# Additions of a state-space layer and of an index stage moved from VectorE to GpSimd

## The chip, the cores and the metric

The kernel runs on one core of one Trainium2 chip. The metric is the device time of one execution in microseconds (us). Engines are named as in the profile: PE is TensorE's matmul and PEld its weight load, DVE is VectorE, ACT is ScalarE, POOL is GpSimd, SP is SyncE, which here only issues loads.

## The reference

A decoder trunk of two layers on 256 tokens of width 1024, in float32. Layer 0 mixes with attention and a gating unit, layer 1 with an S5 state-space layer and a GLU; each is followed by a PEER layer of 8 heads with 16 experts a head and token. Cut to what the change touches:

```python
# S5, for every group of 16 channels: 64 complex states, a scan over the tokens
xr = jnp.einsum('bsgc,gpc->bsgp', u, bbr)
xi = jnp.einsum('bsgc,gpc->bsgp', u, bbi)
_, _, sr, si = lax.associative_scan(combine, (a_r, a_i, xr, xi), axis=1)
# PEER: the 16 best pairs of 16 x 16 candidates, as rows of a table of 16384 experts
cand = sv[:, :, 0, :, None] + sv[:, :, 1, None, :]
cidx = si[:, :, 0, :, None] * PEER_NKEYS + si[:, :, 1, None, :]
cs, cpos = lax.top_k(cand.reshape(t, PEER_HEADS, -1), PEER_TOPK)
idx = jnp.take_along_axis(cidx.reshape(t, PEER_HEADS, -1), cpos, axis=-1)
act = gelu(einsum('td,tkd->tk', xbb, u_tab[ib]));  y = einsum('tk,tkd->td', gb * act, v_tab[ib])
```

## The kernel before

Two tiles of 128 tokens, two layers and eight heads give 32 groups of routing and expert work (`GROUPS`), n = 0 to 31, of 16 experts each: 512 steps g. Each engine runs the same list of steps in order. In step g GpSimd gathers one row of 2048 float32 (u and v of one expert) for each of 128 tokens, 1 MB, into one of nine buffers (`RING`, line 463); VectorE multiplies the u half with `h` and sums it (`dot_product`, L1324); ScalarE makes a gate weight and a diagonal of it (L661 to L667); TensorE multiplies the v half with that diagonal (`expert`, L920). The gather of step g waits until the expert of step g - 9 is done (`v_done`).

All other work hangs in a table `WORK`, written out by hand in `between()`: at a step, an engine first runs its part of the stages that stand there and then that step's expert work. Group n's routing begins at step `ROUTE_AT[n]`; `ROUTE` gives the stages' offsets from there (keys 0, pairs 2, best 4, exp 6, index 6, gate 8). S5 works in 8 chunks of 128 channels for each token tile t, nine steps apart, from step 128 (t + 1) + 11: `s5_rot` at slot + 1, `s5_add` at slot + 2, `s5_scan` at slot + 3, `s5_back` at slot + 5, `s5_out` (TensorE) at slot + 6.

- `s5_rot` multiplies the input in PSUM by a table of cosines and one of sines (L1213, L1214), `s5_add` turns them into the real and the imaginary part (L1218, L1219: 128x512 each), `s5_scan` runs two scans (L1231), and `s5_back` turns back (L1240, L1242). All of it is on VectorE, with a drain (VectorE waits until it has finished) between dependent steps.
- `route_index` makes the 16 indices of a group: positions split into row and column (L1298, L1299), a one-hot comparison (L1301), a product with the keys' indices (L1304), a sum over 16 (L1306) and the combination (L1308), which releases `idx_ok`. GpSimd waits for `idx_ok` at the first gather of a group, ScalarE in `q_keep` before it overwrites scores.
- GpSimd has, apart from one mask at the start (L452), only the gathers.

Of the kernel before, what the change touches and what calls it, by code (L numbers as in the profile page):

```python
# [19 lines left out]
ALU = mybir.AluOpType  # L20
# [49 lines left out]

ROUTE = (("route_keys", 0), ("route_pairs", 2), ("route_best", 4), ("route_exp", 6), ("route_index", 6),
         ("route_gate", 8))
ROUTE_AT = {1: 0, 2: 16, 3: 26, 4: 40, 5: 50, 6: 72, 7: 80, 8: 88, 9: 96, 10: 104, 11: 112, 12: 120, 13: 134, 14: 150,
            15: 166, 16: 234, 17: 242, 18: 250, 19: 260, 20: 276, 21: 292, 22: 308, 23: 324, 24: 362, 25: 370, 26: 378,
            27: 400, 28: 416, 29: 432, 30: 448, 31: 464}
ROUTE_ALL = [(name, 0) for name, _ in ROUTE]


PRELUDE = [("norm_T", 0), ("hT_copy", 0), ("norm_sq", 0), ("norm_ms", 0), ("norm_sd", 0), ("norm_r", 0),
# [13 lines left out]
def between():  # L95
# [3 lines left out]
    def at(n, slot, *stages):  # L99
        work[n + slot // TOPK].setdefault(slot % TOPK, []).extend(stages)  # L100
# [57 lines left out]
    for t in range(T):  # L158
        g = PH * (t + 1)
        at(g, 2, ("y_sum", 2 + 2 * t))  # L160
        mix_norm(g, 3, 4 + 2 * t)
        at(g, 3, ("s5_turns", t, 0))
        at(g, 4, ("s5_frac", t, 0))
        at(g, 6, ("s5_tables", t, 0))
        for c in range(KC):
            slot = 11 + 9 * c
            at(g, slot - 1 if c == 0 else slot - 6, ("s5_in", t, c))
            at(g, slot, ("s5_decay", t, c))
            at(g, slot + 1, ("s5_rot", t, c))
            at(g, slot + 2, ("s5_add", t, c))  # L170
            at(g, slot + 3, ("s5_scan", t, c))
            at(g, slot + 4, ("s5_cmat", t, c))
            at(g, slot + 5, ("s5_back", t, c))
            if c + 1 < KC:
                at(g, slot + 3, ("s5_turns", t, c + 1))
                at(g, slot + 4, ("s5_frac", t, c + 1))
                at(g, slot + 6, ("s5_tables", t, c + 1))
            at(g, slot + 6, ("s5_out", t, c))
            if c % 4 == 3:
                at(g, slot + 8, ("s5_gelu", t, c // 4))  # L180
        for b in range(2):
# [24 lines left out]
def trunk(nc, x_in, vecs, cols_in, cst_in, w_in, sgu_g, sgu_wT, sgu_bT, w_out, s5_par, s5_b, s5_c, glu_w, wq, skT, uv_tab,  # L206
          out):
    with ExitStack() as ctx:
# [51 lines left out]
        def part(start, size, pattern="p (a s) -> p a s", **dims):  # L260
# [187 lines left out]
        @block.gpsimd  # L448
        def _(pool):
            pool.wait_ge(ld_sgu, 48)  # L450
            sg3 = sgw[:, :].rearrange("p (h i) -> p h i", h=8)
            nc.gpsimd.affine_select(out=sg3, in_=sg3, pattern=[[0, 8], [1, P]], compare_op=ALU.is_ge, fill=0.0, base=0,  # L452
                                    channel_multiplier=-1).then_inc(sgm_ok, 1)

            for g in range(GROUPS * TOPK):
                n, s = g // TOPK, g % TOPK
                if s == 0:
                    pool.wait_ge(idx_ok, n + 1)
                if g < RING and g % 2 == 0:
                    pool.wait_ge(z_done, 6 + g // 2)  # L460
                if g >= RING:
                    pool.wait_ge(v_done, g - RING + 1)
                nc.gpsimd.indirect_dma_start(  # L463
                    out=ring[g % RING], out_offset=None, in_=uv_tab,
                    in_offset=bass.IndirectOffsetOnAxis(ap=idx[n % AHEAD][:, s:s + 1], axis=0)).then_inc(got[g % RING], 16)

# [478 lines left out]
        def _(dve):  # L945
# [268 lines left out]
                V.tensor_tensor(by_sin, x4, sin, ALU.mult).then_inc(w_ok, 1)  # L1214
                dve.drain()

            def s5_add(t, c):
                V.tensor_tensor(by_cos[:, 0, :, :], by_cos[:, 0, :, :], by_sin[:, 1, :, :], ALU.add)  # L1218
                V.tensor_tensor(by_cos[:, 1, :, :], by_cos[:, 1, :, :], by_sin[:, 0, :, :], ALU.subtract)  # L1219
                dve.drain()  # L1220
                if t == 1:

                    V.tensor_tensor(by_cos[:, :, :, 0], by_cos[:, :, :, 0], z_last[:, :, 4 * c:4 * c + 4], ALU.add)
                    dve.drain()

            def s5_scan(t, c):

                dve.wait_ge(dt5_ok, KC * t + c + 1)
                for r in range(2):
                    w = by_cos[:, r, :, :].rearrange("p j s -> p (j s)")  # L1230
# [19 lines left out]
                xs = x[:, t, cols_]  # L1250
                V.scalar_tensor_tensor(xs, gate[:, cols_], 0.5, xs, ALU.mult, ALU.add).then_inc(x_done, 1)

            hot = cand[:, :].rearrange("p (a k) -> p a k", k=TOPK)
            hot2 = cand[:, :].rearrange("p (i a k) -> p i a k", i=2, k=TOPK)

            def route_keys(n):

# [22 lines left out]
            def route_best(n):  # L1280

                top_cs = cs[n % 2]
                V.max(top_cs[:, 0:8], cand_a)
                V.tensor_scalar(top_f[:, 0, :], top_i[:, 0, :], float(NK * (n // (T * PH))), None, ALU.add)
                V.tensor_copy(top_f[:, 1, :], top_i[:, 1, :])
                dve.drain()
                V.max_index(pos_i[:, 0:8], top_cs[:, 0:8], cand_a)
# [4 lines left out]
                dve.drain()  # L1292
                V.max_index(pos_i[:, 8:16], top_cs[:, 8:16], cand_b).then_inc(cs_ok, 1)
                dve.drain()

            def route_index(n):

                V.tensor_scalar(pos_ab[:, 0, :], pos_i[:, :], 4, None, ALU.logical_shift_right)  # L1298
                V.tensor_scalar(pos_ab[:, 1, :], pos_i[:, :], 15, None, ALU.bitwise_and)  # L1299
                dve.drain()  # L1300
                V.tensor_tensor(hot, bc(pos_ab[:, :, :].rearrange("p i a -> p (i a)"), [None, TOPK]),  # L1301
                                bc(iota16, [2 * TOPK, None]), ALU.is_equal)
                dve.drain()
                V.tensor_tensor(hot2, hot2, top_f[:, :, :].unsqueeze(2).to_broadcast([P, 2, TOPK, TOPK]), ALU.mult)  # L1304
                dve.drain()
                V.tensor_reduce(row[:, :, :].rearrange("p i a -> p (i a)"), hot, AX.X, ALU.add)  # L1306
                dve.drain()
                V.scalar_tensor_tensor(idx[n % AHEAD][:, :], row[:, 0, :], float(NK), row[:, 1, :], ALU.mult,  # L1308
                                       ALU.add).then_inc(idx_ok, 1)

            def route_gate(n):
# [7 lines left out]
            def dot_product(g):  # L1319
# [11 lines left out]
                         s5_frac=s5_frac, s5_add=s5_add, s5_scan=s5_scan, s5_back=s5_back, glu_sum=glu_sum, norm_r=norm_r)  # L1331
            stage |= dict(route_keys=route_keys, route_pairs=route_pairs, route_best=route_best, route_index=route_index,
                          route_gate=route_gate)

            def run(stages):
# [85 lines left out]
```

## Time and profile before

| | |
|---|---|
| median of 3 runs | 1553.74 us (1551.52 to 1554.93) |
| the profiled execution, its own time | 1553.37 us |
| its span, first to last instruction | 1551.6 us |
| busy: PE, DVE, ACT, POOL | 1097.8, 1111.5, 770.2, 589.4 us |
| DMA moved | 603.39 MB, 389 GB/s on average |
| indirect gathers | 512, 536.90 MB, 84.8% of 16 DMA engines' span |

The page gives busy times of the engines, then the span in 40 slices (busy share in tenths, DMA share and GB/s), then the chain that ended last and the costliest groups of instructions. A group's row reads: line, engine, operation, output <- input with shapes, count, busy us in total, mean ns of one, idle time of the engine before them and what ended it.

### The profile page before, as it was taken

How to read it: one execution, taken by the hardware profiler on the slowest of the kernel's cores; microseconds unless marked ns; L12 is line 12 of the kernel's file. 1: busy time of each engine (PE TensorE's matmuls, PEld its weight loads, DVE VectorE, ACT ScalarE, POOL GpSimd, SP SyncE). 2: the span in 40 equal slices, each digit the busy share in tenths (PEclk: the TensorE clock that was granted, in tenths of full speed). 3: DMA queues.
4: the chain of work that ended last, by engine and by line, in shares of the span. 5: the costliest groups of instructions: out<-in, count | busy, mean ns of one | idle time of the engine just before them, and what ended most of it. 6: DMA issues, size and time to landing. Idle time of an engine off the chain costs nothing.

```text
span 1551.6 us, 19133 instructions
## 1 busy us (share of the span) xinstructions
PE 1097.8 (71%) x5920; PEld 348.4 (22%) x5920; DVE 1111.5 (72%) x2533; ACT 770.2 (50%) x2120; POOL 589.4 (38%) x517
## 2 busy tenths in 40 slices
PE   7997678866765666679866575656878666666665
PEld 3542222322211212223221121212323111111110
DVE  2356887479787899985477799999456866666554
ACT  2315554445456667764334666766334644444433
POOL 0024343323443354554334345344432443434430
PEclk9998689878966776879988567686998777676675
DMA  9569999999999998999999999999999999999995
GB/s 358 179 234 413 420 405 418 414 415 408 415 421 421 354 374 358 410 421 415 412 413 414 403 357 369 355 363 406 380 416 415 415 422 421 421 421 421 421 422 234
DMA packets 105418, 603.39 MB, mean 389 GB/s; under 512 B 9314, under 2 KB 9442, under 8 KB 39780
## 3 DMA queue, kind: packets, MB, share of 16 engines
q0 software_dynamic: 73728, 536.90, 84.8%
q1 hardware_dynamic: 31588, 65.26, 11.3%
q8 instruction: 47, 0.77, 0.2%
q14 instruction: 55, 0.45, 0.1%
HBM read 601.08 MB, written 1.05 MB: 388 GB/s over the span
## 4 chain that ended last, share of the span: by engine, by line
DMA 32%; DVE 31%; PE 22%; ACT 7%; issue 3%; DVEq 3%; ACTq 1%; POOL 1%; SPq 0%; POOLq 0%
DMA rings<-in_uv_tab_dram,idx 24%; DVE rings L1324 11%; PE ps L715 9%; PE ps L920 8%; DMA wst<-in_wq_dram 7%; DVE mem L1231 2%; PE ps L908 2%; DVE dgs L1324 2%; ACT dgs L667 1%; DVE mem L1213 1%; ACT wgt L664 1%; DMA rings<-in_w_in_dram 1%; DVE mem L1242 1%; ACT L661 1%; DVE mem L1240 1%
## 5 line engine op out<-in xcount | busy, mean ns | idle before, releaser
L920 PE MATMUL ps<-rings,dgs 64*64 64x512 f32 x3648 | 638.0, 804 | 343.3 <-ACT dgs L667 342.6
L463 POOL DMA_INDIRECT rings<-in_uv_tab_dram,idx x456 | 521.7, 1144 | 804.3 <-PE ps L920 687.8
L1324 DVE CUSTOM_DVE_ANT_0 rings<-rings,h 128x1024 f32<-128x1024 f32 x456 | 550.7, 1224 | 210.8 <-DMA rings<-in_uv_tab_dram,idx 197.7
L661 ACT ACTIVATE gel<-dots 128x1 f32<-128x1 f32 x512 | 102.1, 199 | 522.2 <-DVE dots L1324 518.5
L920 PEld LDWEIGHTS ps<-rings,dgs 64*64 64x64 f32 x3648 | 128.3, 163 | 783.4 <-ACT dgs L667 682.3
L667 ACT ACTIVATE dgs<-cst,wgt 128x128 f32<-128x128 f32 x512 | 205.6, 402 | 36.3 <-issue 1.5
L715 PE MATMUL ps<-wst,hT 128*128 128x512 f32 x320 | 168.0, 666 | 37.1 <-DMA wst<-in_wq_dram 20.5
L664 ACT ACTIVATE wgt<-gel,share 128x1 f32<-128x1 f32 x512 | 150.8, 295 | 35.5 <-issue 0.3
L920 PE MATMUL ps<-dgs 64*64 64x512 f32 x448 | 80.2, 795 | 53.2 <-ACT dgs L667 53.1
L463 POOL DMA_INDIRECT dgs<-in_uv_tab_dram,idx x56 | 65.9, 1176 | 88.3 <-PE ps L920 74.8
L715 PEld LDWEIGHTS ps<-wst,hT 128*128 128x128 f32 x320 | 63.4, 212 | 138.1 <-issue 134.9
L1324 DVE CUSTOM_DVE_ANT_0 dgs<-dgs,h 128x1024 f32<-128x1024 f32 x56 | 68.5, 1223 | 26.5 <-DMA dgs<-in_uv_tab_dram,idx 24.5
L661 ACT ACT_TABLE_LOAD x56 | 71.8, 1283 | 3.8 <-DVE dots L1324 2.2
L715 PE MATMUL ps<-rings,hT 128*128 128x512 f32 x128 | 59.0, 611 | 3.7 <-DMA rings<-in_w_in_dram 2.8
L1324 DVE DVE_READ_ACCUMULATOR2_ANT dots<- 128x1 f32 x512 | 42.6, 83 | 0.0
L648 ACT ACT_TABLE_LOAD x31 | 39.8, 1283 | 0.8
L920 PEld LDWEIGHTS ps<-dgs 64*64 64x64 f32 x448 | 14.2, 156 | 106.9 <-ACT dgs L667 101.2
L1231 DVE TENSOR_TENSOR_SCAN mem<-mem 128x512 f32<-128x512 f32 x32 | 37.4, 1210 | 0.0
L556 ACT ACTIVATE mem<-ps 128x512 f32<-128x512 f32 x16 | 9.5, 594 | 53.6 <-PE ps L715 53.6
L715 PEld LDWEIGHTS ps<-rings,hT 128*128 128x128 f32 x128 | 24.4, 197 | 33.2 <-issue 33.1
L1108 DVE COPY mem<-ps 128x512 f32<-128x512 f32 x16 | 11.0, 689 | 27.4 <-PE ps L707 27.4
L908 PE MATMUL ps<-wst,hT 128*128 128x512 f32 x64 | 29.6, 605 | 0.0
(192 smaller groups left out, 991.2 us busy)
## 6 DMA issues: line engine op xcount, KB each, us to landing
wst<-in_wq_dram SPq DMA_DIRECT2D x15, 2048.0 KB, 28.2
wst<-in_w_out_dram SPq DMA_DIRECT2D x4, 2048.0 KB, 22.8
wst<-in_glu_w_dram SPq DMA_DIRECT2D x4, 2048.0 KB, 31.7
rings<-in_uv_tab_dram,idx POOLq DMA_INDIRECT x456, 15.7
rings<-in_w_in_dram SPq DMA_DIRECT2D x3, 2048.0 KB, 16.7
rings<-in_w_in_dram SPq DMA_DIRECT2D x2, 1024.0 KB, 7.5
dgs<-in_w_in_dram SPq DMA_DIRECT2D x1, 2048.0 KB, 19.4
vec<-in_vecs_dram SPq DMA_DIRECT2D x3, 512.0 KB, 17.2
```

What stands on the lines that cost most here:

```text
L463: nc.gpsimd.indirect_dma_start(out=ring[g % RING], out_offset=None, in_=uv_tab, in_offset=bass.IndirectOffsetOnAxis(ap=idx[n % AHEAD][:, s ...
L648: A.activation(gexp[n % 2][:, :], cs[n % 2][:, :], ACT.Exp, bias=ncs[n % 2], accum_out=gsum[n % 2]).then_inc(exp_ok, 1)
L661: A.activation(gel[i][:, every], dots[i][:, every], ACT.Gelu_apprx_tanh)
L664: A.activation(wgt[i][:, c], gel[i][:, c], ACT.Copy, scale=share[n % AHEAD][:, c])
L667: A.activation(diag[:, (g + k) % DIAGS, :], ident, ACT.Copy, scale=wgt[i][:, c]).then_inc(diag_ok, 1)
L715: ins = PE.matmul(ps[:, bank, :], lhs[:, k, :], rhs[:, k, :], start=(k == 0), stop=(k == KC - 1))
L908: ins = PE.matmul(ps[:, 2 + b, :], hTs[t][:, k, :], wst[:, w % 2, k, :], start=False, stop=(k == KC - 1))
L920: ins = PE.matmul(ps[64 * b:64 * b + 64, 4 + 2 * t + half, :], diag[rows, g % DIAGS, rows], ring[g % RING][rows, D + b * BANK:D + (b + 1) ...
L1213: V.tensor_tensor(by_cos, x4, cos, ALU.mult)
L1231: ins = V.tensor_tensor_scan(w, decay.rearrange("p j s -> p (j s)"), w, 0.0, ALU.mult, ALU.add)
L1240: V.tensor_tensor(by_sin, by_cos, sin, ALU.mult).then_inc(d_ok, 1)
L1324: V.tensor_tensor_reduce(out=u, in0=u, in1=h[:, t, :], scale=1.0, scalar=0.0, op0=ALU.mult, op1=ALU.add, accum_out=dots[n % 2][:, s:s + 1] ...
```

## The change

- `s5_add` moves from VectorE to GpSimd. It waits for `w_ok` (the second product of `s5_rot`), and its second addition increments `add_ok`, for which `s5_scan` now waits. `s5_scan` moves from slot + 3 to slot + 4. The small addition for t = 1 goes into `s5_scan`.
- `route_index` is taken apart. The split of positions and the comparison go to the end of `route_best` on VectorE (two steps earlier). For n > 0 the product is GpSimd's (`index_key`, offset 6), and the sum over 16 becomes four halvings there, of 256, 128, 64 and 32 elements a partition (`index_half`, offset 7; `index_end`, offset 8), then a sum of 16 and a copy to the integer tile. Each of them waits for the semaphore `hop_ok` that the one in front increments. The factor 128 moves to a small operation on VectorE that was there. Group 0 keeps the old form (`route_first`).
- The one-hot tile is a new one, `hot_p`, and `route_best` of group n waits for the indices of group n - 1.
- GpSimd runs the stages of step g - 6 (`POOL_LAG`) in front of the gather of step g.

```diff
+POOL_LAG = 6
-ROUTE = (("route_keys", 0), ("route_pairs", 2), ("route_best", 4), ("route_exp", 6), ("route_index", 6),
-         ("route_gate", 8))
+ROUTE = (("route_keys", 0), ("route_pairs", 2), ("route_best", 4), ("route_exp", 6), ("index_key", 6),
+         ("route_gate", 8), ("index_half", 7), ("index_end", 8))
...
-            at(g, slot + 3, ("s5_scan", t, c))
+            at(g, slot + 4, ("s5_scan", t, c))
...
+            def s5_add(t, c):
+
+                pool.wait_ge(w_ok, KC * t + c + 1)
+                nc.gpsimd.tensor_tensor(by_cos[:, 0, :, :], by_cos[:, 0, :, :], by_sin[:, 1, :, :], ALU.add)
+                nc.gpsimd.tensor_tensor(by_cos[:, 1, :, :], by_cos[:, 1, :, :], by_sin[:, 0, :, :],
+                                        ALU.subtract).then_inc(add_ok, 1)
...
+            def halve(n, step, w):
+
+                pool.wait_ge(hop_ok, 6 * (n - 1) + step)
+                nc.gpsimd.tensor_tensor(hot[:, :, 0:w], hot[:, :, 0:w], hot[:, :, w:2 * w], ALU.add).then_inc(hop_ok, 1)
+
+            def index_key(n):
+
+                pool.wait_ge(pos_ok, n)
+                nc.gpsimd.tensor_tensor(hot2, hot2, top_f[:, :, :].unsqueeze(2).to_broadcast([P, 2, TOPK, TOPK]),
+                                        ALU.mult).then_inc(hop_ok, 1)
+
+            def index_half(n):
+                halve(n, 1, 8)
+                halve(n, 2, 4)
+
+            def index_end(n):
+                halve(n, 3, 2)
+                halve(n, 4, 1)
+                pool.wait_ge(hop_ok, 6 * (n - 1) + 5)
+                nc.gpsimd.tensor_tensor(hot2[:, 0, :, 0], hot2[:, 0, :, 0], hot2[:, 1, :, 0], ALU.add).then_inc(hop_ok, 1)
+                pool.wait_ge(hop_ok, 6 * n)
+                nc.gpsimd.tensor_copy(idx[n % AHEAD][:, :], hot2[:, 0, :, 0]).then_inc(idx_ok, 1)
...
             for g in range(GROUPS * TOPK):
                 n, s = g // TOPK, g % TOPK
+                if g >= POOL_LAG:
+                    run(WORK[(g - POOL_LAG) // TOPK].get((g - POOL_LAG) % TOPK, []))
                 if s == 0:
                     pool.wait_ge(idx_ok, n + 1)
...
-            def s5_add(t, c):
-                V.tensor_tensor(by_cos[:, 0, :, :], by_cos[:, 0, :, :], by_sin[:, 1, :, :], ALU.add)
-                V.tensor_tensor(by_cos[:, 1, :, :], by_cos[:, 1, :, :], by_sin[:, 0, :, :], ALU.subtract)
-                dve.drain()
+            def s5_scan(t, c):
+
+                dve.wait_ge(add_ok, KC * t + c + 1)
                 if t == 1:
...
                 V.max(top_cs[:, 0:8], cand_a)
-                V.tensor_scalar(top_f[:, 0, :], top_i[:, 0, :], float(NK * (n // (T * PH))), None, ALU.add)
+                if n:
+                    dve.wait_ge(idx_ok, n)
+                V.tensor_scalar(top_f[:, 0, :], top_i[:, 0, :], float(NK * (n // (T * PH))), float(NK), ALU.add, ALU.mult)
...
                 V.max_index(pos_i[:, 8:16], top_cs[:, 8:16], cand_b).then_inc(cs_ok, 1)
                 dve.drain()
-
-            def route_index(n):
-
                 V.tensor_scalar(pos_ab[:, 0, :], pos_i[:, :], 4, None, ALU.logical_shift_right)
                 V.tensor_scalar(pos_ab[:, 1, :], pos_i[:, :], 15, None, ALU.bitwise_and)
                 dve.drain()
-                V.tensor_tensor(hot, bc(pos_ab[:, :, :].rearrange("p i a -> p (i a)"), [None, TOPK]),
-                                bc(iota16, [2 * TOPK, None]), ALU.is_equal)
-                dve.drain()
+                ins = V.tensor_tensor(hot, bc(pos_ab[:, :, :].rearrange("p i a -> p (i a)"), [None, TOPK]),
+                                      bc(iota16, [2 * TOPK, None]), ALU.is_equal)
+                if n:
+                    ins.then_inc(pos_ok, 1)
+                dve.drain()
+
+            def route_first(n):
+
                 V.tensor_tensor(hot2, hot2, top_f[:, :, :].unsqueeze(2).to_broadcast([P, 2, TOPK, TOPK]), ALU.mult)
                 dve.drain()
                 V.tensor_reduce(row[:, :, :].rearrange("p i a -> p (i a)"), hot, AX.X, ALU.add)
```

## Rows read from the trace of the kernel before

**Rows 1.** The page: busy times, and two rows of the span's 40 slices.

```profile
PE 1097.8 (71%) x5920; PEld 348.4 (22%) x5920; DVE 1111.5 (72%) x2533; ACT 770.2 (50%) x2120; POOL 589.4 (38%) x517
...
DVE  2356887479787899985477799999456866666554
...
GB/s 358 179 234 413 420 405 418 414 415 408 415 421 421 354 374 358 410 421 415 412 413 414 403 357 369 355 363 406 380 416 415 415 422 421 421 421 421 421 422 234
```

**Rows 2.** Stretches: busy PE, PEld, DVE, ACT, POOL; PE clock, DMA share, GB/s.

```profile
505.00:660.00 155.00, 99.30 (x784) 34.43 (x784) 144.50 (x269) 105.27 (x291) 70.94 (x56) 0.73 0.95 374
...
855.00:1095.00 240.00, 156.07 (x1082) 50.01 (x1082) 212.25 (x438) 156.50 (x426) 102.10 (x81) 0.71 0.95 373
1240.00:1480.00 240.00, 156.58 (x780) 27.27 (x776) 156.90 (x373) 101.00 (x309) 100.94 (x98) 0.69 1.01 421
```

**Rows 3.** DVE's waits for gathers (us, times, longest): first 855:1095, then 1240:1480.

```profile
DVE rings L1324 <- DMA rings<-in_uv_tab_dram,idx: 0.2, 1, 0.2
...
DVE rings L1324 <- DMA rings<-in_uv_tab_dram,idx: 66.7, 57, 1.6
```

**Rows 4.** DVE in order of time (start us, us): index end; turn and additions.

```profile
562.70 0.69 DVE L1304 TENSOR_TENSOR cand<-cand,top_f 128x512 f32<-128x512 f32 x1
...
564.31 1.22 DVE L1324 CUSTOM_DVE_ANT_0 rings<-rings,h 128x1024 f32<-128x1024 f32 x1
...
567.74 1.22 DVE L1214 TENSOR_TENSOR mem<-ps,mem 128x1024 f32<-128x1024 f32 x1
...
570.57 0.69 DVE L1218 TENSOR_TENSOR mem<-mem 128x512 f32<-128x512 f32 x1
...
571.98 1.22 DVE L1324 CUSTOM_DVE_ANT_0 rings<-rings,h 128x1024 f32<-128x1024 f32 x1
```

**Rows 5.** Both engines in order of time: a gather's issue beside DVE instructions.

```profile
567.79 0.93 POOL L463 DMA_INDIRECT rings<-in_uv_tab_dram,idx  x1 [0.30 <-issue]
...
1028.11 1.23 DVE L1242 TENSOR_TENSOR mem<-mem 128x1024 f32<-128x1024 f32 x1
1028.16 1.98 POOL L463 DMA_INDIRECT rings<-in_uv_tab_dram,idx  x1 [1.80 <-PE ps L920]
...
1029.25 1.22 DVE L1324 CUSTOM_DVE_ANT_0 rings<-rings,h 128x1024 f32<-128x1024 f32 x1
```

**Rows 6.** The gathers' issues grouped, in 855:1095 and then in 1240:1480.

```profile
L463 POOL DMA_INDIRECT rings<-in_uv_tab_dram,idx x72 | 91.8, 1276 | 118.9 <-PE ps L920 107.5 <-DVE idx L1308 6.1 <-issue 5.3
...
L463 POOL DMA_INDIRECT rings<-in_uv_tab_dram,idx x87 | 89.5, 1029 | 127.0 <-PE ps L920 121.8 <-issue 5.3
```

**Rows 7.** GpSimd's elementwise groups of the whole span: mask, one preset.

```profile
L452 POOL TENSOR_SCALAR_AFFINE_SELECT sgw<-sgw 128x1024 f32<-128x1024 f32 x1 | 1.6, 1593 | 37.5 <-DMA sgb<-in_sgu_bT_dram 37.5
...
L1411 POOL MEMSET const-float32-1.0<- 128x1 f32 x1 | 0.1, 104 | 0.0
```

**Rows 8.** One line's instructions in 505:660 and 855:1095: L1218, then L1304.

```profile
505.00:660.00 155.00, 4.19 (x6) 0.73 0.95 374
855.00:1095.00 240.00, 5.50 (x8) 0.71 0.95 373
...
505.00:660.00 155.00, 2.08 (x3) 0.73 0.95 374
855.00:1095.00 240.00, 3.46 (x5) 0.71 0.95 373
```

**Rows 9.** DVE's groups with two SBUF inputs in 855:1095: first and last of eleven.

```profile
L1324 DVE CUSTOM_DVE_ANT_0 rings<-rings,h 128x1024 f32<-128x1024 f32 x74 | 88.6, 1223 | 3.6 <-DMA rings<-in_uv_tab_dram,idx 0.2
...
L1276 DVE TENSOR_TENSOR cand<-top 128x256 f32<-128x256 f32 x5 | 2.0, 406 | 0.0
```

**Rows 10.** Instructions up to 600 us: line 463 (POOL), then line 1324 (DVE).

```profile
0.00:600.00 600.00, 201.04 (x178) 0.83 0.94 376
...
0.00:600.00 600.00, 205.14 (x339) 0.83 0.94 376
```

**Rows 11.** The view of DMA issues: gathers, median us from issue to landing.

```profile
rings<-in_uv_tab_dram,idx POOLq DMA_INDIRECT x456, 15.7
```

More of the change, by code:

```diff
@@ L77 @@
             27: 400, 28: 416, 29: 432, 30: 448, 31: 464}
-ROUTE_ALL = [(name, 0) for name, _ in ROUTE]
+ROUTE_ALL = [("route_first" if name == "index_key" else name, 0) for name, _ in ROUTE[:6]]
 PRELUDE = [("norm_T", 0), ("hT_copy", 0), ("norm_sq", 0), ("norm_ms", 0), ("norm_sd", 0), ("norm_r", 0),
@@ L288, in trunk @@
         row = sb("row", [P, 2, TOPK])
+        hot_p = sb("hot_p", [P, 512])
         idx = [sb(f"idx{i}", [P, TOPK], U32) for i in range(AHEAD)]
@@ L322, in trunk @@
         r_ok, rd_ok, sn_done, dt5_ok, dd_ok = (sem(n) for n in ("r_ok", "rd_ok", "sn_done", "dt5_ok", "dd_ok"))
+        add_ok = sem("add_ok")
+        pos_ok, hop_ok = sem("pos_ok"), sem("hop_ok")
         sq_done, ms_done, sd_done, h_done, nT_done, hT_act, hT_dve, x_done, w_used = (sem(n) for n in (
@@ L453, in _, with run @@
                                     channel_multiplier=-1).then_inc(sgm_ok, 1)
+            def s5_add(t, c):
[3 more added lines that the diff above has]
+                                        ALU.subtract).then_inc(add_ok, 1)
+            hot = hot_p[:, :].rearrange("p (a k) -> p a k", k=TOPK)
+            hot2 = hot_p[:, :].rearrange("p (i a k) -> p i a k", i=2, k=TOPK)
+            def halve(n, step, w):
[15 more added lines that the diff above has]
+                nc.gpsimd.tensor_copy(idx[n % AHEAD][:, :], hot2[:, 0, :, 0]).then_inc(idx_ok, 1)
+            stage = dict(s5_add=s5_add, index_key=index_key, index_half=index_half, index_end=index_end)
+            def run(stages):
+                for name, *args in stages:
+                    if name in stage:
+                        stage[name](*args)
             for g in range(GROUPS * TOPK):
                 n, s = g // TOPK, g % TOPK
+                if g >= POOL_LAG:
+                    run(WORK[(g - POOL_LAG) // TOPK].get((g - POOL_LAG) % TOPK, []))
                 if s == 0:
@@ L1224, in s5_add @@
                     dve.drain()
-            def s5_scan(t, c):
                 dve.wait_ge(dt5_ok, KC * t + c + 1)
@@ L1251, in glu_sum @@
                 V.scalar_tensor_tensor(xs, gate[:, cols_], 0.5, xs, ALU.mult, ALU.add).then_inc(x_done, 1)
-            hot = cand[:, :].rearrange("p (a k) -> p a k", k=TOPK)
-            hot2 = cand[:, :].rearrange("p (i a k) -> p i a k", i=2, k=TOPK)
+            hot = hot_p[:, :].rearrange("p (a k) -> p a k", k=TOPK)
+            hot2 = hot_p[:, :].rearrange("p (i a k) -> p i a k", i=2, k=TOPK)
             def route_keys(n):
@@ L1307, in route_index @@
                 dve.drain()
-                V.scalar_tensor_tensor(idx[n % AHEAD][:, :], row[:, 0, :], float(NK), row[:, 1, :], ALU.mult,
+                V.scalar_tensor_tensor(idx[n % AHEAD][:, :], row[:, 0, :], 1.0, row[:, 1, :], ALU.mult,
                                        ALU.add).then_inc(idx_ok, 1)
@@ L1330, in _ @@
                          s5_b0=s5_b0, s5_b1=s5_b1, s5_rot=s5_rot,
-                         s5_frac=s5_frac, s5_add=s5_add, s5_scan=s5_scan, s5_back=s5_back, glu_sum=glu_sum, norm_r=norm_r)
-            stage |= dict(route_keys=route_keys, route_pairs=route_pairs, route_best=route_best, route_index=route_index,
+                         s5_frac=s5_frac, s5_scan=s5_scan, s5_back=s5_back, glu_sum=glu_sum, norm_r=norm_r)
+            stage |= dict(route_keys=route_keys, route_pairs=route_pairs, route_best=route_best, route_first=route_first,
                           route_gate=route_gate)
```

## The prediction

> **What bounds the kernel now.** I read the page first, then two tables of stretches, then VectorE's waits. The page puts VectorE in front (1111.5 us) with PE beside it, and the slices show that it isn't the same everywhere: in most of them the DMA moves 410 to 422 GB/s, in two hollows (slices 14 to 17 and 23 to 28) 342 to 385 or so, and there VectorE's digits are 8 and 9 [rows 1]. The hollows are the S5 stages of the two token tiles. Cut out, they are 505 to 660 us and 855 to 1095 us: VectorE busy 144.5 of 155 and 212.3 of 240, DMA 374 and 373 GB/s; a stretch without S5 has 421 GB/s with VectorE at 157 of 240 [rows 2]. The waits say the same: in the second hollow VectorE waits 0.2 us for a gather, in the quiet stretch 66.7 us [rows 3]. So VectorE sets the pace in 395 us, and the gathers' DMA in nearly all the rest, where nothing that the change saves or adds on VectorE counts as long as a few us of GpSimd's delay don't empty the DMA queue. The floor under a gain is the DMA's own pace: at 421 GB/s the bytes of the hollows take 155 x 374/421 = 137.7 us and 240 x 373/421 = 212.6 us, so at most 17.3 + 27.4 = 44.7 us are to be had.
>
> **What VectorE loses in work.** The two additions of a chunk: from the start of the first (570.57) to the next dot (571.98) are 1.41 us [rows 4]. The end of the index stage: from the product (562.70) to the next dot (564.31) are 1.61 us, drains included [rows 4]. In the hollows lie 6 + 8 chunks and 3 + 5 index stages [rows 8]: 14 x 1.41 = 19.7 us and 8 x 1.61 = 12.9 us, together 32.6 us, under the floor in each hollow. The other 2 chunks and 23 index stages (group 0 keeps its own) lie where the DMA sets the pace: nothing. Splitting positions and comparing only move two steps earlier on the same engine: nothing. The second factor on a 16-wide operation and the product for the first group: nothing that a row could show.
>
> **What the work costs on GpSimd, and whom it blocks.** This decides the case. A gather's issue takes 0.93 us beside the products from PSUM (567.79, VectorE's L1214 running). At 1028.16 it takes 1.98 us: VectorE had begun a product of two SBUF tensors at 1028.11, which ended at 1029.34, and the issue ended 0.80 us behind it, though the next dot, again with two SBUF inputs, ran from 1029.25 [rows 4, 5]. So GpSimd waits for a VectorE instruction that has two SBUF inputs, gets in as that ends, and needs the way only for a moment. The mean issue is 1276 ns in the second hollow and 1029 ns in the quiet stretch [rows 6], which fits. Does the reverse hold, VectorE waiting for GpSimd? The issue reads one column of indices, and the dot beside it shows nothing (1.22 us). An addition reads 2 x 512 elements a partition.
>
> The Trainium skill, SBUF — State Buffer, section Who interferes with whom, says that a VectorE instruction with two SBUF inputs and a GpSimd instruction that reads SBUF exclude each other for the whole instruction, whichever starts first. The trace agrees for one direction (0.93 against 1.98 us); for the other it has no row. By that rule the change buys VectorE's time with VectorE's own waits.
>
> I take the block as real both ways, since one way is measured. Its price is the length c of a GpSimd operation of 512 elements with two inputs. The only elementwise rows are a mask with one input, 1593 ns for 1024 elements, and a preset of one element, 104 ns [rows 7]. Halved, the mask gives 0.80 us, the lower end; if the two inputs are read one after the other, 1.60 us, the upper end. I take 1.0, nearer to the row. The Trainium skill, GPSIMD Engine Reference, section Performance versus the Vector engine, has 4497 ns for an addition of 2048 elements, an estimate of 1.12 us for 512; the sum below would be 2.2 us for a chunk's additions at full block instead of 2.0 and end some 4 us later.
>
> How often does VectorE want the way in that time? In the second hollow its eleven groups with two SBUF inputs fill 164.6 of 240 us, 0.69 [rows 9]. Behind a turn it is more, since dots follow it: 0.85 is my estimate. Then:
> - additions: 2 x 1.0 x 0.85 = 1.70 us of waiting against 1.41 us saved, +0.29 us, x 14 = +4.1 us;
> - index: the product of 512 is 1.0 us, the halvings, the last sum and the copy are 512 elements together, 0.9 us, with 0.1 us for each of 6 short operations in place of the one counted in c, about 2.5 us in all; x 0.69 = 1.73 against 1.61 saved, +0.12 us, x 8 = +1.0 us.
>
> That is +5.1 us with c = 1.0. With c = 0.80: (1.36 - 1.41) x 14 and (2.1 x 0.69 - 1.61) x 8 give -0.7 - 1.3 = -2.0 us. With c = 1.60: (2.72 - 1.41) x 14 and (3.7 x 0.69 - 1.61) x 8 give 18.3 + 7.5 = +26 us. Some of a loss is taken up where the first hollow runs out into full DMA, so I put +4.5 us on the profiled execution's 1553.4 us (span 1551.6, within 0.4 us of the median): 1558 us.
>
> **New waits and what queues behind them.** On GpSimd: at 600 us it has issued 178 gathers and VectorE has done 339 / 2, some 169.5 dots [rows 10], so it is 8 steps ahead. With the lag of 6 it stands in front of a chunk's addition about one step before VectorE has turned that chunk, waits, works 2 us and perhaps waits out one or two dots. Behind it wait the gathers, 4 to 6 us late. A step in the hollow is 240 us over 84 dots, 2.86 us; eight steps are 22.9 us, a gather lands 15.7 us after its issue [rows 11]: 7 us of room. Cost nothing; without that room each late gather would cost its lateness. In the quiet stretch a step is 2.5 us and the queue is full for 15.7 us, so 4 to 6 us of delay leave it full. GpSimd's own load, for nine steps: 9 x 1.28 + 0.3 between issues = 14 us, additions with waits 5, index stages 5; 24 of 25.7 us. It is close. On VectorE: `s5_scan` waits for `add_ok` behind three dots (3.45 us, 5.4 with two blocks of 1.0), against 1.2 + 1.0 + 1.2 + 1.0 = 4.4 us for the additions at worst: nothing. `route_best` waits for the group before; routing starts are at least 8 steps apart, GpSimd is 8 ahead and finishes at offset 8 + 6 = 14, VectorE asks at 8 + 4 = 12 and GpSimd is then at 20: nothing. ScalarE's `q_keep` and the first gather of each group want indices that come no later than offset 14 of at least 16; nothing. SP's loads wait for products of TensorE and don't change.
>
> **The rivals.**
> - A: VectorE isn't blocked; the way is held for a read only, as the issues' reads are. For it: the dot beside the issue at 1028.16 is as long as any. Against: that read is one column. VectorE gets back 32.6 us, less some 5 where other waits step in (PE for the transposed input, ScalarE's tables): 1553.4 - 28 = 1525 us.
> - B, slower: the additions read their two inputs one after the other and hold VectorE for all of it, c = 1.6: place, the 22 stages in the hollows; price +26 us, 1579 us. It decides against the change from 2 x c x 0.85 = 1.41, c = 0.83 us on. Beside it GpSimd's load for nine steps passes 25.7 us, and it would set the pace. For it: two streams through what the gathers show to be one way. Against: nothing says that they don't overlap.
> - C: a partial block. VectorE slips in at the gaps between GpSimd's operations and pays half: 0.85 + 0.86 us against 1.41 + 1.61: -0.56 x 14 - 0.75 x 8 = -14 us, 1540 us.
> - D: the change moves nothing, because VectorE's relief in the hollows is eaten by weight loads in the same DMA queues: 1553 us.
>
> **How the numbers follow.** Likeliest 0.42: full block at c between 0.8 and 1.25, 1552 to 1568 us. A 0.16, B 0.18, C 0.18, D 0.06. A measurement tells 0.2% (3 us) from no change. Faster: A, C and a little of the likeliest, 0.37. Same: D and a part of the likeliest, 0.20. Slower: the rest of the likeliest and B, 0.43. The range must reach into A and into B: 1527 to 1577 us leaves out about 2 in 10. Signs are mixed; the likeliest case's own range is 1552 to 1568.
>
> **What would show it.** Right: dots (L1324) and scans longer than 1.22 us or with gaps in front of them exactly while a GpSimd addition runs; additions around 1.0 us when free and up to 2.2 when a dot runs; both hollows as long as before within a few us; the quiet stretches still at 421 GB/s. A would show dots at 1.22 us beside running additions and the hollows at 400 GB/s. B would show additions of 1.6 us and more and the hollows at 360 GB/s, with GpSimd busy throughout. The prediction fails if GpSimd's short operations cost much more than 0.1 us each, or if late gathers show up as VectorE waiting for DMA in the hollows.

## The result and the profile after

The changed kernel takes 1582.55 us (median, 1579.6 to 1585.9) against 1554.34 us for the kernel before in the same comparison: a ratio of 1.0186, 95% interval 1.0173 to 1.0198. It is 28 us slower, where 1558 us were forecast and 1577 us was the upper end of the range. The page of the kernel after, the lines that answer to [rows 1]:

```profile
span 1582.3 us, 19187 instructions
PE 1086.2 (69%) x5920; PEld 349.7 (22%) x5920; DVE 1115.8 (71%) x2408; ACT 768.0 (49%) x2120; POOL 813.3 (51%) x766
...
GB/s 360 185 239 379 420 416 417 414 415 390 405 420 420 304 408 319 391 411 413 415 412 416 380 357 340 328 306 371 413 415 394 376 421 422 421 420 422 420 421 258
```

VectorE executes 125 instructions fewer (2533 to 2408) and is busy 4 us longer. GpSimd has gained 224 us. The hollows are deeper. The stretches of the kernel after (columns as in [rows 2]), taken where its own S5 stages and quiet part lie:

```profile
505.00:675.00 170.00, 104.22 (x796) 36.10 (x800) 146.09 (x250) 108.67 (x303) 114.66 (x90) 0.72 0.90 360
870.00:1125.00 255.00, 156.91 (x1099) 53.22 (x1100) 219.27 (x410) 157.01 (x429) 156.94 (x133) 0.73 0.90 352
1275.00:1510.00 235.00, 145.02 (x750) 25.91 (x744) 157.74 (x353) 97.33 (x299) 125.31 (x130) 0.70 1.01 421
```

The quiet part still has 421 GB/s, the hollows 360 and 352 instead of 374 and 373 [rows 2]. Comparing the start of the same gather in both traces tells where the time went: 12 us between steps 144 and 192, 15 between 280 and 320, 12 between 368 and 384, the last outside both hollows. The stretches between them and behind step 384 give back some 7 us in all.

Groups of the kernel after, three of VectorE's and then four of GpSimd's new ones (columns as in [rows 9]):

```profile
L1370 DVE CUSTOM_DVE_ANT_0 rings<-rings,h 128x1024 f32<-128x1024 f32 x456 | 594.6, 1324 | 212.4 <-DMA rings<-in_uv_tab_dram,idx 200.2 <-issue 0.5
...
L1342 DVE TENSOR_TENSOR hot_p<-pos_ab,cst 128x512 f32<-128x512 uint32 x32 | 22.2, 693 | 2.4
L1363 DVE TENSOR_SCALAR share<-gexp,tiny 128x16 f32<-128x16 f32 x32 | 15.9, 496 | 2.5
...
L477 POOL TENSOR_TENSOR hot_p<-hot_p,top_f 128x512 f32<-128x512 f32 x31 | 41.2, 1330 | 35.3 <-DVE hot_p L1342 35.1
L472 POOL TENSOR_TENSOR hot_p<-hot_p 128x128 f32<-128x128 f32 x31 | 31.5, 1016 | 2.4
L463 POOL TENSOR_TENSOR mem<-mem 128x512 f32<-128x512 f32 x16 | 27.3, 1707 | 0.0
L462 POOL TENSOR_TENSOR mem<-mem 128x512 f32<-128x512 f32 x16 | 22.5, 1404 | 3.2 <-DVE mem L1260 3.0
```

The dots from `rings` took 1224 ns before (550.7 us over the 456); now their mean is 1324 ns, 44 us more in all. One chunk in order of time, both engines (start, duration, engine, line):

```profile
956.47 1.22 DVE L1370 CUSTOM_DVE_ANT_0 dgs<-dgs,h 128x1024 f32<-128x1024 f32 x1
...
957.38 1.44 POOL L462 TENSOR_TENSOR mem<-mem 128x512 f32<-128x512 f32 x1
...
957.62 2.28 DVE L1370 CUSTOM_DVE_ANT_0 rings<-rings,h 128x1024 f32<-128x1024 f32 x1
...
958.78 2.25 POOL L463 TENSOR_TENSOR mem<-mem 128x512 f32<-128x512 f32 x1
...
961.06 0.17 DVE L1268 TENSOR_TENSOR mem<-mem,z_last 128x8 f32<-128x8 f32 x1 [1.15 <-POOL mem L463]
```

The first addition waits until the dot of 956.47 ends and then runs. The dot of 957.62 can't start its work until that addition is done: 2.28 us instead of 1.22. The second addition meanwhile waits for that dot and takes 2.25 us instead of 1.26. And VectorE, three dots behind its turn, stands 1.15 us until the second addition is done.

Small operations of VectorE can fare worse. This one, of 16 elements, takes 0.23 us before the change; here it starts 0.01 us before the first addition and ends behind the second, 2.55 us later:

```profile
900.11 2.55 DVE L1363 TENSOR_SCALAR share<-gexp,tiny 128x16 f32<-128x16 f32 x1
900.12 1.27 POOL L462 TENSOR_TENSOR mem<-mem 128x512 f32<-128x512 f32 x1
901.35 1.26 POOL L463 TENSOR_TENSOR mem<-mem 128x512 f32<-128x512 f32 x1
```

It happens three times in the hollows of the changed kernel (3.14, 2.55 and 3.10 us) and adds about 8 us to VectorE's work there.

### The profile page after: what moved, and what is told of

Its sections match the earlier page's. It is cut to its first block, busy times and chain, and to the rows that moved or that the text cites. A ratio compares the mean times of both kernels' runs of the same rounds, so it can differ in the third digit from the quotient of the medians.

```text
span 1582.3 us, 19187 instructions
## 1 busy us (share of the span) xinstructions
PE 1086.2 (69%) x5920; PEld 349.7 (22%) x5920; DVE 1115.8 (71%) x2408; ACT 768.0 (49%) x2120; POOL 813.3 (51%) x766
## 3 DMA queue, kind: packets, MB, share of 16 engines
q0 software_dynamic: 73728, 536.90, 83.5%
q1 hardware_dynamic: 31588, 65.26, 11.1%
## 4 chain that ended last, share of the span: by engine, by line
DMA 28%; PE 24%; DVE 23%; ACT 9%; POOL 6%; DVEq 4%; issue 4%; ACTq 2%; SPq 0%; POOLq 0%
DMA rings<-in_uv_tab_dram,idx 23%; PE ps L761 11%; PE ps L966 9%; DVE rings L1370 8%; DMA wst<-in_wq_dram 5%; POOL rings L509 3%; PE ps L954 2%; ACT L707 2%; ACT dgs L713 1%; ACT wgt L710 1%; DVE mem L1273 1%; DVE dgs L1370 1%; DVE mem L1284 1%; POOL mem L463 1%; ACTq L649 1%
## 5 line engine op out<-in xcount | busy, mean ns | idle before, releaser
L966 PE MATMUL ps<-rings,dgs 64*64 64x512 f32 x3648 | 620.9, 786 | 354.7 <-ACT dgs L713 353.9
L509 POOL DMA_INDIRECT rings<-in_uv_tab_dram,idx x456 | 528.9, 1160 | 593.5 <-PE ps L966 473.4
L1370 DVE CUSTOM_DVE_ANT_0 rings<-rings,h 128x1024 f32<-128x1024 f32 x456 | 594.6, 1324 | 212.4 <-DMA rings<-in_uv_tab_dram,idx 200.2
L761 PE MATMUL ps<-wst,hT 128*128 128x512 f32 x320 | 169.0, 670 | 37.6 <-ACT scr L612 20.7
L966 PE MATMUL ps<-dgs 64*64 64x512 f32 x448 | 84.2, 832 | 83.4 <-ACT dgs L713 83.4
L509 POOL DMA_INDIRECT dgs<-in_uv_tab_dram,idx x56 | 72.2, 1289 | 58.2 <-PE ps L966 48.3
L1370 DVE CUSTOM_DVE_ANT_0 dgs<-dgs,h 128x1024 f32<-128x1024 f32 x56 | 76.0, 1358 | 30.4 <-DMA dgs<-in_uv_tab_dram,idx 28.8
L472 POOL TENSOR_TENSOR hot_p<-hot_p 128x256 f32<-128x256 f32 (+1 forms) x124 | 94.0, 758 | 6.1
L477 POOL TENSOR_TENSOR hot_p<-hot_p,top_f 128x512 f32<-128x512 f32 x31 | 41.2, 1330 | 35.3 <-DVE hot_p L1342 35.1
```

Source lines behind the costliest of these rows:

```text
L472: nc.gpsimd.tensor_tensor(hot[:, :, 0:w], hot[:, :, 0:w], hot[:, :, w:2 * w], ALU.add).then_inc(hop_ok, 1)
L477: nc.gpsimd.tensor_tensor(hot2, hot2, top_f[:, :, :].unsqueeze(2).to_broadcast([P, 2, TOPK, TOPK]), ALU.mult).then_inc(hop_ok, 1)
L509: nc.gpsimd.indirect_dma_start(out=ring[g % RING], out_offset=None, in_=uv_tab, in_offset=bass.IndirectOffsetOnAxis(ap=idx[n % AHEAD][:, s ...
L761: ins = PE.matmul(ps[:, bank, :], lhs[:, k, :], rhs[:, k, :], start=(k == 0), stop=(k == KC - 1))
L966: ins = PE.matmul(ps[64 * b:64 * b + 64, 4 + 2 * t + half, :], diag[rows, g % DIAGS, rows], ring[g % RING][rows, D + b * BANK:D + (b + 1) ...
L1370: V.tensor_tensor_reduce(out=u, in0=u, in1=h[:, t, :], scale=1.0, scalar=0.0, op0=ALU.mult, op1=ALU.add, accum_out=dots[n % 2][:, s:s + 1] ...
```

## The experiments

Two theories were set against each other. Theory 1: GpSimd's SBUF reads and VectorE's instructions with two SBUF inputs shut each other out, and VectorE pays. Theory 2: GpSimd's queue, which issues the gathers in order, is held up by the new work. All ratios are to the kernel before, run on the same chip.

**Each half alone.** `s5_only` leaves the index stage on VectorE at its old offset, `index_only` leaves S5 as before.

```diff
-            stage = dict(s5_add=s5_add, index_key=index_key, index_half=index_half, index_end=index_end)
+            stage = dict(s5_add=s5_add)
...
-            stage = dict(s5_add=s5_add, index_key=index_key, index_half=index_half, index_end=index_end)
+            stage = dict(index_key=index_key, index_half=index_half, index_end=index_end)
```

> Only the S5 additions on GpSimd (and the scan one step later); the index stage is VectorE's, at its old offset. Theory 1 (block): a GpSimd operation that reads SBUF and a VectorE instruction with two SBUF inputs shut each other out, and VectorE pays for it. The trace of the changed kernel has the free additions at 1.26 us, so 14 chunks x (2 x 1.26 x 0.85 - 1.41) = +10 us, with dots longer than 1.3 us only near additions, and the wait of the scan for the additions as an extra: 1564 to 1572 us. Theory 2 (queue): what costs is GpSimd's own order, gathers that go out late behind additions and index operations; additions alone hold GpSimd for 2.5 us in 16 places, and VectorE gets 20 us back: 1540 to 1555 us.

Measured 1567.32 us, ratio 1.0089 (1.0072 to 1.0106), +13.4 us.

> Only the end of the index stage on GpSimd; S5 is as before. Theory 1 (block): a stage's seven operations are 3.5 us when free, so in the hollows 8 x (3.5 x 0.69 - 1.61) = +6 us, and outside them nearly nothing as long as the DMA sets the pace: 1557 to 1564 us. Theory 2 (queue): seven operations, each held up by dots and each behind the one before, delay the gathers of three steps in 31 places, also where weights are streamed (+11 us at steps 352 to 384 in the changed kernel): 1565 to 1580 us.

Measured 1562.55 us, ratio 1.0056 (1.0039 to 1.0073), +8.6 us. Both halves cost, each within what theory 1 expected. Together they make 22 of the 28 us.

**GpSimd's work without the change.** The kernel before is left as it is; GpSimd gets private operations at the same steps. In `own_read` they read a constant tile, in `own_write` they only write. Those of the index stage wait for the 16 best pairs (`cs_ok`), not for the comparison.

```diff
+            def own(size):
...
+                nc.gpsimd.tensor_tensor(own_t[:, 0:size], cst[:, P:P + size], cst[:, 2 * P:2 * P + size],
+                                        ALU.add).then_inc(own_ok, 1)
...
+            def private_add(t, c):
+
+                pool.wait_ge(w_ok, KC * t + c + 1)
+                own(512)
+                own(512)
...
+WIDTHS = {512: (640, 512), 256: (640,), 128: (400,), 64: (200,), 32: (120,), 16: (80,)}
...
+                    nc.gpsimd.memset(own_t[:, 0:width], 0.0).then_inc(own_ok, 1)
```

> The kernel before, VectorE's work untouched and waiting for nothing new, with GpSimd running additions of the same sizes at the same steps, from a constant tile into a private tile. Whatever this costs is the price of the operations alone. Theory 1: 14 x 2 x 1.26 x 0.85 + 8 x 3.5 x 0.69 = +30 + 19 = up to +49 us less what full DMA takes up: 1585 to 1603 us, dots beside them up to 2.5 us. Theory 2: the delay of gathers alone, as large as in the changed kernel, whose VectorE was 32 us lighter: 1575 to 1590 us, and own_write gives the same.

> As own_read, but each addition is replaced by one or two memsets of about the same length on GpSimd, which write and read nothing. GpSimd's queue is held as long and gathers are as late; no SBUF read of GpSimd meets VectorE. Theory 1: the dots stay at 1.22 us and the time at that of before, 1551 to 1558 us. Theory 2: the same time as own_read, over 1570 us.

Measured: `own_read` 1601.26 us, ratio 1.0307 (1.029 to 1.0324), +47.3 us; `own_write` 1556.93 us, ratio 1.0017 (1.0008 to 1.0027), +3.0 us. VectorE's groups, first of `own_read` (dots, scan, the comparison, the one-input sum), then the dots of `own_write` and two of its memsets:

```profile
L1368 DVE CUSTOM_DVE_ANT_0 rings<-rings,h 128x1024 f32<-128x1024 f32 x456 | 581.6, 1294 | 181.1 <-DMA rings<-in_uv_tab_dram,idx 167.7 <-issue 0.5
...
L1275 DVE TENSOR_TENSOR_SCAN mem<-mem 128x512 f32<-128x512 f32 x32 | 43.1, 1386 | 0.0
...
L1345 DVE TENSOR_TENSOR cand<-pos_ab,cst 128x512 f32<-128x512 uint32 x32 | 31.5, 984 | 2.4
...
L1350 DVE TENSOR_REDUCE row<-cand 128x32 f32<-128x512 f32 x32 | 22.0, 686 | 2.3
```

```profile
L1368 DVE CUSTOM_DVE_ANT_0 rings<-rings,h 128x1024 f32<-128x1024 f32 x456 | 550.7, 1224 | 219.9 <-DMA rings<-in_uv_tab_dram,idx 207.2 <-issue 0.5
...
L466 POOL MEMSET own_t<- 128x640 f32 x94 | 60.1, 640 | 23.2 <-DVE pos_i L1337 17.3 <-DVE mem L1258 4.7
L466 POOL MEMSET own_t<- 128x512 f32 x63 | 33.0, 524 | 3.6
```

A pair of memsets holds GpSimd 0.64 + 0.52 = 1.16 us, an addition that nothing stands in the way of 1.26 us; yet with the memsets the dots stay at 1224 ns and the kernel is 3 us slower in all, and with the additions the dots grow, as do the scans (1210 to 1386 ns) and the comparison (695 to 984). The sum with one input (686 ns) doesn't. That is theory 1.

One gap is left: the additions wait for VectorE in their turn, so `own_read` holds GpSimd's queue longer than `own_write` (217 against 131 us for the private work), and later gathers could be part of its 47 us. The waits say no. In the stretches 505 to 675 and 870 to 1125 us VectorE of `own_read` never waits for a gather (2.6 us if the second is followed to 1155 us, where that kernel's S5 stages end), that of `own_write` 6.3 us. So theory 2 has no part in the hollows at this lag: there VectorE pays by its own longer instructions.

**What VectorE's relief is worth.** `relief` takes both jobs away from VectorE and gives them to nobody; `relief_own_read` adds `own_read`'s operations to it.

```diff
-                V.tensor_tensor(by_cos[:, 0, :, :], by_cos[:, 0, :, :], by_sin[:, 1, :, :], ALU.add)
-                V.tensor_tensor(by_cos[:, 1, :, :], by_cos[:, 1, :, :], by_sin[:, 0, :, :], ALU.subtract)
-                dve.drain()
...
-                V.tensor_tensor(hot2, hot2, top_f[:, :, :].unsqueeze(2).to_broadcast([P, 2, TOPK, TOPK]), ALU.mult)
-                dve.drain()
-                V.tensor_reduce(row[:, :, :].rearrange("p i a -> p (i a)"), hot, AX.X, ALU.add)
-                dve.drain()
-                V.scalar_tensor_tensor(idx[n % AHEAD][:, :], row[:, 0, :], float(NK), row[:, 1, :], ALU.mult,
+                V.scalar_tensor_tensor(idx[n % AHEAD][:, :], top_f[:, 0, :], float(NK), top_f[:, 1, :], ALU.mult,
```

> The kernel before with the work simply left out: neither VectorE nor GpSimd does the two S5 additions (L1218, L1219) nor the product and the sum of the index stage (L1304, L1306); the indices are then the keys in order, without the positions. It measures what VectorE's relief is worth if nobody pays for it. If VectorE sets the pace in the two hollows as the prediction says: 14 x 1.41 + 8 x 1.5 = 31.7 us less a few us for other waits, 1520 to 1530 us. If something else (PE, ScalarE, weight loads) is right behind VectorE: 1538 to 1553 us.

Measured 1529.26 us, ratio 0.9846 (0.9828 to 0.9865): -24.6 us. Its gathers fetch other rows of the table than before; the quiet slices still move 421 GB/s.

> relief and own_read in one kernel: VectorE does neither the additions nor the product and sum, GpSimd runs additions of the same sizes at the same steps on tiles of its own, and VectorE waits for none of them. It is the changed kernel without VectorE's new waits for GpSimd (work left out as in relief). If block and relief add up: 1554 - 24.6 + 47.3 = 1577 us. If the changed kernel's new waits (18.7 us for the additions) are on the path: 1560 to 1572 us. If they are not: 1577 to 1585 us, as the changed kernel.

Measured 1574.67 us, ratio 1.0133 (1.011 to 1.0157), between what was expected if the new waits count and if they don't. So the +28 us of the change come apart as -24.6 for the relief, 1574.67 - 1529.26 = +45.4 for GpSimd's reads, and 1582.55 - 1574.67 = +7.9 for the rest. The last is a difference between kernels of two comparisons and good to about 3 us. It isn't the price of VectorE's waits for GpSimd's results alone, because the private operations meet other instructions than the real ones: they add 84.5 us to VectorE's busy time (1050.7 in `relief`, 1135.2 us), where the changed kernel has 65.1 us more than `relief` (1115.8).

**Places alone.** `sched_only` has the changed kernel's places with all work on VectorE.

```diff
-            stage = dict(s5_add=s5_add, index_key=index_key, index_half=index_half, index_end=index_end)
+            stage = {}
```

> All work on VectorE, but at the places of the changed kernel: scan one step later, positions and comparison at the end of the stage at offset 4. If the new places cost nothing, as the prediction says: 1551 to 1557 us. If the order itself is at fault (the waits for ScalarE's exponentials at L1361 in the changed kernel, 11.8 us against 4.7): 1558 to 1566 us.

Measured 1554.24 us, ratio 1.0006 (0.9996 to 1.0016): the new places cost nothing.

**How far ahead GpSimd stands.** `lag4` and `lag8` move its stages in its queue; `scan_late` moves the scan away from the additions.

```diff
-POOL_LAG = 6
+POOL_LAG = 4
...
-POOL_LAG = 6
+POOL_LAG = 8
...
-            at(g, slot + 4, ("s5_scan", t, c))
+            at(g, slot + 6, ("s5_scan", t, c))
...
-            at(g, slot + 5, ("s5_back", t, c))
+            at(g, slot + 7, ("s5_back", t, c))
...
-            at(g, slot + 6, ("s5_out", t, c))
+            at(g, slot + 8, ("s5_out", t, c))
```

> The changed kernel with GpSimd's stages two gathers earlier in its queue (POOL_LAG 4). In the changed kernel the first addition began at a median of 3.3 us behind the turn, since GpSimd stood at a gather whose buffer was not free, and the scans waited 18.7 us for the additions. If these waits are on the path: they go to under 5 us, 1564 to 1574 us. If only the block matters: 1579 to 1586 us. If late gathers matter, GpSimd now waits for VectorE in front of more gathers: over 1590 us.

Measured 1601.21 us, ratio 1.0314 (1.0295 to 1.0333).

> The changed kernel with GpSimd's stages two gathers later in its queue (POOL_LAG 8). Lag 4 cost 18.7 us more, with 153.6 us in front of the index product in place of 35.1. If GpSimd's waits in front of gathers are what lag trades: under 10 us there, and more than 30 us of VectorE waiting for additions: between 1576 and 1592 us. If late gathers were half of the loss: 1568 to 1576 us.

Measured 1605.05 us, ratio 1.0334 (1.0317 to 1.0352).

> The changed kernel with the scan at slot + 6, the turn back at slot + 7 and the product at slot + 8 (before: + 4, + 5, + 6), so that VectorE has five dots in place of three between turn and scan. The waits for the additions (18.7 us) should go to under 3 us. If they are on the path: 1564 to 1572 us. If the wait only takes the place of idle time further on: 1579 to 1586 us.

Measured 1604.92 us, ratio 1.0336 (1.0316 to 1.0356). The waits (who <- for whom, us in total, times, longest), first of the kernel after, then of `lag4`, of `lag8` and of `scan_late`:

```profile
DVE rings L1370 <- DMA rings<-in_uv_tab_dram,idx: 200.2, 154, 2.7
...
POOL hot_p L477 <- DVE hot_p L1342: 35.1, 21, 3.0
...
DVE mem L1273 <- POOL mem L463: 12.9, 6, 3.5
...
DVE mem L1268 <- POOL mem L463: 5.8, 3, 3.5
```

```profile
DVE rings L1370 <- DMA rings<-in_uv_tab_dram,idx: 236.8, 171, 4.3
...
POOL hot_p L477 <- DVE hot_p L1342: 153.6, 28, 9.4
...
POOL mem L462 <- DVE mem L1260: 56.6, 15, 7.7
```

```profile
DVE mem L1273 <- POOL mem L463: 40.4, 7, 7.1
DVE mem L1268 <- POOL mem L463: 31.8, 7, 6.5
```

```profile
DVE mem L1232 <- ACT mem L639: 27.5, 15, 2.6
...
DVE mem L1259 <- PE ps L932: 16.1, 8, 4.0
```

With lag 4 VectorE no longer waits for an addition, but GpSimd stands 210 us (after: 38) in front of its operations with gathers queued behind, and VectorE waits 37 us more for gathers: 19 us slower. With lag 8 it is the other way round: 72 us of VectorE waiting for additions (after: 19), and 22 us slower. Of the three lags tried 6 is the best, with some 20 us lost on either side. For lag 4 the reading with late gathers came true (over 1590 us), and the table of its waits shows theory 2's mechanism at work, which lag 6 avoids; lag 8 lies above both of its forecasts, and so does `scan_late`. `scan_late` removed the waits for the additions and brought two others, for the whole part of the next table (L1232, 27.5 us against 3.4), which the scan had covered, and for the product that now ends late (L1259). It therefore tells nothing about what the 19 us of waiting for additions in the changed kernel are worth.

**Inside the hollows or outside.** `index_in` gives GpSimd the end of the index stage for the eight groups in or beside the hollows, `index_out` for the other 23; both have S5 as before.

```diff
+ON_POOL = [n for n in range(1, 32) if n in (13, 14, 15, 19, 20, 21, 22, 23)]
...
+ON_POOL = [n for n in range(1, 32) if n not in (13, 14, 15, 19, 20, 21, 22, 23)]
```

> index_only with the end of the index stage on GpSimd for the eight groups 13 to 15 and 19 to 23 alone, whose routing lies in or beside the two hollows; the other groups' is VectorE's. If what index_only cost (+8.6 us) is paid in the hollows, as the prediction's sum has it: 1560 to 1563 us. If it is paid elsewhere: 1552 to 1557 us.

Measured 1560.23 us, ratio 1.004 (1.0026 to 1.0053), +6.4 us.

> The reverse: GpSimd for the other 23 groups, which the prediction put at nothing because the DMA sets the pace there. If that is right: 1551 to 1556 us. If the block and the later gathers also cost where VectorE has idle time (steps 32 to 64 and 368 to 384 lost about 5 us each in index_only): 1559 to 1563 us.

Measured 1558.09 us, ratio 1.0027 (1.0017 to 1.0038), +4.3 us: outside the hollows the work isn't free, at 0.2 us a stage against 0.8 inside. The result lies between its two forecasts. The loss isn't spread evenly: by the starts of the gathers `index_out` loses 7 us between steps 368 and 384 and gives most of it back later, where `s5_only` loses 1 us. So the index stages cause the changed kernel's loss at this place.

**Another way to unload the hollows.** `reroute` and `reroute2` are the kernel before with other steps at which routing begins, and no work on another engine.

```diff
-ROUTE_AT = {1: 0, 2: 16, 3: 26, 4: 40, 5: 50, 6: 72, 7: 80, 8: 88, 9: 96, 10: 104, 11: 112, 12: 120, 13: 134, 14: 150,
-            15: 166, 16: 234, 17: 242, 18: 250, 19: 260, 20: 276, 21: 292, 22: 308, 23: 324, 24: 362, 25: 370, 26: 378,
+ROUTE_AT = {1: 0, 2: 16, 3: 26, 4: 40, 5: 50, 6: 72, 7: 80, 8: 88, 9: 96, 10: 104, 11: 112, 12: 120, 13: 134, 14: 208,
+            15: 220, 16: 234, 17: 242, 18: 250, 19: 258, 20: 276, 21: 300, 22: 332, 23: 344, 24: 362, 25: 370, 26: 378,
```

(This is `reroute2`; `reroute` has 13 at 128, 22 at 330 and 23 at 342.)

> The kernel before with nothing moved to another engine: the routing of groups 13 to 15 and 19 to 23 begins at steps 128, 208, 220 and 258, 276, 300, 330, 342 in place of 134, 150, 166 and 260, 276, 292, 308, 324, so that fewer of the stages, about 10 us of VectorE each, lie in the hollows and more where VectorE has idle time. If VectorE's work in the hollows is what counts, wherever else it goes: 2 or 3 stages leave the first hollow and 2 the second, up to 17 and 20 us: 1522 to 1540 us. If the stages cost as much where they go to: 1551 to 1560 us.

Measured 1543.18 us, ratio 0.9932 (0.9914 to 0.9951), -10.7 us and between its two forecasts.

> As reroute, but group 13 stays at step 134 (reroute lost 6.8 us at steps 128 to 144, where its routing met the normalisation), and groups 22 and 23 begin at 332 and 344. If the loss there was the collision: 1534 to 1541 us. If group 13 costs as much in the hollow: 1541 to 1548 us.

Measured 1535.85 us, ratio 0.9888 (0.987 to 0.9906): 17.7 us faster than the kernel before and 46.7 us than the changed one. Its hollows, in the stretches of [rows 2]:

```profile
505.00:660.00 155.00, 107.00 (x840) 36.84 (x843) 137.23 (x209) 107.01 (x306) 77.32 (x62) 0.75 0.97 393
855.00:1095.00 240.00, 163.36 (x1164) 55.71 (x1164) 211.43 (x420) 156.66 (x432) 107.31 (x87) 0.77 0.97 389
```

The DMA now moves 393 and 389 GB/s there. VectorE's work was not reduced (1110.4 us against 1111.5); it went to steps where VectorE had been idle. How much of the 7 us between `reroute` and `reroute2` is group 13 and how much groups 22 and 23 was not taken apart.

## Why the prediction was wrong

**Right.** What bounds the kernel, and where: `relief` gave back 24.6 us, against 32.6 us of work and 28 us with other waits taken off (rival A's sum); that leaves nothing of D. The block in both directions: GpSimd waits for a two-input instruction of VectorE as the issue at 1028.16 did [rows 5], and VectorE waits for GpSimd's whole operation, as the dot of 957.62 and `own_read` against `own_write` show. The Trainium skill, SBUF — State Buffer, section Who interferes with whom, says just this, also that a GpSimd operation that only writes doesn't contend with such an instruction; `own_write` agrees (dots at 1224 ns). The shares 0.85 and 0.69 held too: with the lengths measured below they give 14 x 2.52 x 0.85 + 8 x 3.44 x 0.69 = +49 us for `own_read`, which measured +47.3, some 42 of them in the hollows. New places on VectorE cost nothing (`sched_only`). Direction and mechanism were those of the likeliest case and of B.

Two readings were off and moved no sum. The slices of the hollows hold 354 to 380 GB/s, with edges up to 410, not 342 to 385 [rows 1]. And D's weight loads aren't in the gathers' queue: the page has the gathers on q0 (536.90 MB) and the hardware queue's loads on q1 (65.26 MB).

**Wrong, 1: the price of the operations.** I took c = 1.0 us for 512 elements, nearer to the mask with one input [rows 7], and 2.5 us for an index stage. With nothing in the way an addition takes 1.26 us. The stage takes 1.26 for the product, 0.73, 0.45, 0.30 and 0.25 for the halvings, 0.25 and 0.20 us for the last two, together 3.44 us: 0.2 us and more even for 16 elements, not 0.1, which the prediction had named as a sign of its failing. Put into the prediction's own sum: (2.52 x 0.85 - 1.41) x 14 = +10.2 us and (3.44 x 0.69 - 1.61) x 8 = +6.1 us, 16 us in place of 5. Measured in parts: `s5_only` +13.4, its new waits included, and `index_in` +6.4. The estimate of 1.12 us from the figure of the Trainium skill, GPSIMD Engine Reference, section Performance versus the Vector engine, was nearer than my 1.0, and 0.14 us short. That B's sum of +26 us came close to the result is luck: its price (1.6) isn't true.

**Wrong, 2: nothing outside the hollows.** 23 index stages there cost 4.3 us (`index_out`). In the changed kernel's quiet stretch the DMA stays at 421 GB/s although dots are lengthened; the losses lie where the step-by-step comparison shows them, among them steps 368 to 384, which the index stages cause (`index_out`) and where TensorE waits for weights. Which wait there ends last was not tried.

**Wrong, 3: the scan's wait was costed at nothing.** The step said that GpSimd stands in front of the addition before VectorE has turned the chunk, since it is 8 gathers ahead [rows 10]. A count of issued gathers doesn't say that the engine is free: it was waiting for TensorE to release the buffer of the gather in front. In the changed kernel the first addition began 0.1 to 5.0 us behind its turn, with a median of 3.5 us, and 9 of 16 chunks made VectorE wait, 18.7 us in all. What the changed kernel has beyond reads and relief is +7.9 us. The scan's wait is one reading of it; the three small operations that stood through both additions are another, as no small operation of `relief_own_read` took over 1.8 us. `scan_late`, meant to show the first, didn't, so it stays open what the scan's wait costs.

**The late gathers** were rightly put at nothing at lag 6 (`own_write`, +3.0 us), but the room was smaller than the 7 us worked out from [rows 11]: at lag 4 the same queue cost 19 us.

The corrected sum is 10.2 + 6.1 + 4.3 + 7.9 = +28.5 us against +28 measured. Its last two terms were read from the runs, not foreseen, and that it comes out so well is in part luck: it still counts a relief of 32.6 us where 24.6 were measured, and a block of 49 + 4.3 us where 45.4 were.

## What to carry to other kernels

In this kernel elementwise work that went from VectorE to GpSimd wasn't taken off VectorE, since VectorE mostly ran instructions with two SBUF inputs: each waited out the other, and the slower engine's operation (1.26 us for 0.69 us) was the one that was paid. Before moving work, compare the length on GpSimd, times the share of time in which VectorE wants its second input, with what is saved. Where one engine is the bound only in some stages, moving its work in time can give what moving it between engines can't: here -17.7 us against +28.2 us.

## What the runs showed of the hardware

- The block isn't limited to instructions with two inputs. The small scaling of the gates (L1363, 16 elements, one input and a scalar from SBUF) took 234 ns each time before the change. In the changed kernel its mean is 496 ns and its longest 3.14 us, in `own_read` the mean is 333 and beside the memsets of `own_write` 272 ns. The operation that makes the keys into numbers (L1328) stayed at 174 ns or less in 31 of 32 cases (170 before) and stood 3.10 us once, through a gather's issue and both additions. A reduction of 512 elements was untouched (686 ns).
- The two sides don't fare alike. VectorE can wait out two or three GpSimd operations in a row, as those cases and the instruction at 900.11 show. A gather's issue in the kernel before never waited out two long two-input instructions of VectorE: it takes 0.93 us free and at most 1.99 us with such instructions back to back, and then typically ends 0.80 us behind the end of the first. That it is the reading of the indices that waits is the likely reason, but not shown.
- GpSimd's operations have a floor in these runs: 0.25 us for 32 and for 16 elements with two inputs (0.22 us for 16 in `own_read`), 0.20 with one input, where 512 elements take 1.26.
